# Decays beside the norm, SiLU inside the steps, a gate job behind four others, twelve blocks turned at the stage's end

## What is computed

```python
h = _rmsnorm(x, pre_g)
proj = jnp.einsum('bld,de->ble', h, w_in)
z_ssm, xbc, dt_raw, q, k, v, f_raw, z_att, g_ssm, g_att = jnp.split(proj, ...)
xbc = jax.nn.silu(_causal_dwconv(xbc, conv_w, conv_b))     # 2048 channels, 4 taps
xs, b_ssm, c_ssm = jnp.split(xbc, [1024, 1536], axis=-1)
dt = jax.nn.softplus(dt_raw + dt_bias)                     # 16 heads
a = -jnp.exp(a_log)
y = _ssd_chunked(xs, dt, a, b_ssm, c_ssm, d_skip)          # chunks of 128 tokens
yg = y * jax.nn.silu(z_ssm)
log_f = jax.nn.log_sigmoid(f_raw + fgate_b)                # 16 heads, summed along the tokens later
merged = jax.nn.sigmoid(g_ssm) * p_ssm + jax.nn.sigmoid(g_att) * p_att
```

## Time and profile before

| | us |
|---|---|
| median of 3 runs (3395.37 to 3403.71) | 3396.29 |
| the profiled execution's own time | 3377.47 |
| its span, first to last instruction | 3375.7 |
| TensorE matmul busy | 2890.9 (86%) |
| VectorE busy | 2027.7 (60%) |
| ScalarE busy | 1432.3 (42%) |
| GpSimd busy | 487.1 (14%) |
| mean granted TensorE clock | 0.925 of full |

### The profile page before, as it was taken

The page is one execution under the profiler, slowest core; times in us unless marked ns, Lnnn a source line. Parts: engine busy times, 40 slices in busy tenths (PEclk is TensorE's granted clock), DMA queues, the critical chain, the costliest instruction groups (busy, mean ns, idle before and its releaser), DMA issues. The chain is left out here.

```text
span 3375.7 us, 36680 instructions
## 1 busy us (share of the span) xinstructions
PE 2890.9 (86%) x13236; PEld 2310.3 (68%) x13236; DVE 2027.7 (60%) x2217; ACT 1432.3 (42%) x2086; POOL 487.1 (14%) x407
## 2 busy tenths in 40 slices
PE   6976887999997998799879975967999679999991
PEld 5865666788885766687768853654777568888881
DVE  3774545334443554345433989877345679999993
ACT  3341324333333666343333332343332257777770
POOL 0001310000002767000000000000000014434430
PEclk9986888999997999899989987989999879999996
DMA  3100010112446664112101100010111569999995
GB/s 88 44 19 4 0 36 15 57 50 94 150 143 147 128 134 97 57 51 93 63 20 44 50 14 1 1 38 13 56 44 44 189 246 391 378 378 378 375 338 228
DMA packets 220390, 396.26 MB, mean 117 GB/s; under 512 B 73313, under 2 KB 73441, under 8 KB 220256
## 3 DMA queue, kind: packets, MB, share of 16 engines
q1 hardware_dynamic: 211040, 377.66, 34.0%
q0 software_dynamic: 9216, 16.80, 1.3%
HBM read 356.32 MB, written 54.85 MB: 122 GB/s over the span
## 5 line engine op out<-in xcount | busy, mean ns | idle before, releaser
L2360 DVE TENSOR_TENSOR ex_w<-ex_raw,ex_w 128x2048 fp32r<-128x2048 f32 x192 | 436.6, 2290 | 49.2 <-ACT ex_w L2307 47.4
L2307 ACT ACTIVATE ex_w<-ex_raw 128x2048 fp32r<-128x2048 f32 x192 | 364.6, 1916 | 101.7 <-DMA ex_raw<-in_w_down_e 37.7
L2237 PE MATMUL ps<-ex_w,ex_xT 128*128 128x512 f32 x1536 | 366.7, 395 | 5.3 <-DVE ex_xT L2369 5.0
L2237 PEld LDWEIGHTS ps<-ex_w,ex_xT 128*128 128x128 f32 x1536 | 287.6, 189 | 67.7 <-DVE ex_xT L2369 6.5
L760 DVE TENSOR_TENSOR bs_t<-arena,bs_t 128x1024 fp32r<-128x1024 f32 x80 | 98.1, 1226 | 258.3 <-ACT bs_t L722 258.3
L613 DVE SCALAR_TENSOR_TENSOR arena<-arena,small 128x1023 f32<-128x1023 f32 (+9 forms) x168 | 213.7, 1272 | 4.3
L722 ACT ACTIVATE bs_t<-arena 128x1024 fp32r<-128x1024 f32 x80 | 84.9, 1061 | 296.9 <-PE ps L701 269.6
L699 PE MATMUL ps<-bs_t,bs_w 128*128 128x512 f32 x512 | 200.8, 392 | 11.1 <-DVE bs_w L763 9.0
L1063 POOL TENSOR_TENSOR fa_pl<-fa_p,fa_ph 128x512 fp32r<-128x512 f32 x192 | 191.7, 1012 | 100.8 <-ACT fa_ph L1180 97.9
L700 PE MATMUL ps<-bs_t,bs_w 128*128 128x512 f32 x512 | 200.0, 391 | 0.0
L701 PE MATMUL ps<-bs_t,bs_w 128*128 128x512 f32 x512 | 199.9, 390 | 0.0
(11 more groups left out here) (385 smaller groups left out, 6988.2 us busy)
## 6 DMA issues: line engine op xcount, KB each, us to landing
ex_raw<-in_w_gate_e SPq DMA_DIRECT2D x64, 1024.0 KB, 13.2
ex_raw<-in_w_up_e SPq DMA_DIRECT2D x64, 1024.0 KB, 13.2
ex_raw<-in_w_down_e SPq DMA_DIRECT2D x64, 1024.0 KB, 13.5
arena<-in_w_in SPq DMA_DIRECT2D x108, 512.0 KB, 3.6
arena<-in_x SPq DMA_DIRECT2D x4, 2048.0 KB, 11.2
arena<-in_w_out SPq DMA_DIRECT2D x16, 512.0 KB, 4.3
arena<-expert_out SPq DMA_DIRECT2D x8, 1024.0 KB, 12.2
arena<-in_w_branch_ssm SPq DMA_DIRECT2D x8, 512.0 KB, 3.6
```

The source lines that it names most:

```text
L2237: mm = nc.tensor.matmul(out, l, r, start=(k == 0 and n == 0), stop=(k == kc - 1 and n == 2))
L2307: nc.scalar.activation(half_of(part[m][0], h), raw[m][:, h * W // 2: (h + 1) * W // 2], ACT.Identity).then_inc(high[m], 1)
L2360: V.tensor_tensor(half_of(part[m][1], h), raw[m][:, h * W // 2: (h + 1) * W // 2], half_of(as_f32(part[m][0]), h), ALU.subtract)\
```

## The change

- The six loads of the decays are issued in the norm, behind the taps' and the biases'. In the norm TensorE also computes the logits of token tiles 0 to 4: those of tile t - 1 behind the transposes of tile t. The transposes use six banks in place of eight; bank 7 holds the logits.
- In xbc, the logits of tiles 5 to 7 stand ahead of the first step, and the bias add on VectorE behind them and ahead of its first splits. The small chain runs in steps 0, 2, 4 and 5 on VectorE and 1 and 3 on ScalarE. ScalarE applies SiLU to block b in step 2b + 10.
- xbc has a fifth job, the first half of the gate, which was bs's first job. All taps now lie inside the steps.
- At xbc's end twelve blocks are turned (C is left out), eight copied by VectorE, four (4, 6, 8, 10) by ScalarE, in three slots of two banks; the two sums are computed behind block 2, the exponentials behind the last copy.
- The stages turn of xbc and decays are gone. The forget sums are transposed and copied ahead of z's steps, scanned in its steps 0 to 3, and stored at its end. z's result goes to R(4) in place of R(2).

The core of the diff:

```diff
@@ phase_norm_T, TensorE
-                if n >= 8:
-                    pe.wait_ge(placed, n - 7)
+                if n >= 6:
+                    pe.wait_ge(placed, n - 5)
...
+                if h and 1 <= t <= decays.EARLY:
+                    pe.wait_ge(placed, 2 * t)
+                    decays.logit(pe, t - 1)
@@ class Decays (EARLY = 5)
+    def logit(self, pe, t):
+        n2 = 2 * HEADS
+        if t == 0:
+            pe.wait_ge(self.loaded, 96)
+        for k in range(KC):
+            mm = self.nc.tensor.matmul(self.ps[:, t * n2:(t + 1) * n2], self.hv[:, k, t * P:(t + 1) * P],
+                                       self.w[:, k, :], start=(k == 0), stop=(k == KC - 1))
+        mm.then_inc(self.logits, 1)
+
+    def on_tensor(self, pe):
+        for t in range(self.EARLY, TT):
+            self.logit(pe, t)
+        pe.wait_ge(self.step, 1)
+
+    def on_vector(self, dve):
...
+        dve.wait_ge(self.logits, TT)
+        self.st.then_wait(self.nc.vector.tensor_tensor(
+            v3(x), v3(self.ps), self.bias.unsqueeze(1).to_broadcast([P, TT, 2 * HEADS]), ALU.add))
@@ class TurnedBlocks (BLOCKS = 12, BY_ACT = (4, 6, 8, 10), SUMS = 6)
+    def on_tensor(self, pe, evicted):
+        c, nc, d = self.c, self.nc, self.decays
+        for b in range(self.BLOCKS):
+            slot = b % 3
+            pe.wait_ge(self.silued, b + 1)
+            if b < 3:
+                pe.wait_ge(evicted, XBC // BANK * TT + 2 * b + 2)
+            elif b - 3 in self.BY_ACT:
+                pe.wait_ge(self.by_act, self.BY_ACT.index(b - 3) + 1)
+            else:
+                pe.wait_ge(self.by_vec, self.on_dve.index(b - 3) + 1)
+            for t in range(TT):
+                mm = nc.tensor.transpose(c.ps[:, 2 * slot + t // 4, (t % 4) * P:(t % 4 + 1) * P],
+                                         self.av[:, b, t * P:(t + 1) * P], c.ident[:])
+            mm.then_inc(self.turned, 1)
+            if b == 2:
+                pe.wait_ge(evicted, XBC // BANK * TT + self.SUMS + 1)
+                pe.wait_ge(d.step, d.CHAIN)
+                nc.tensor.matmul(c.ps[:, self.SUMS, 0:P], c.upto[:], d.dta, start=True, stop=True)
+                nc.tensor.matmul(c.ps[:, self.SUMS, P:2 * P], c.ones[:], d.dta, start=True, stop=True)\
+                    .then_inc(self.summed, 1)
...
+    def on_scalar(self, act, tapped):
+        A, d = self.nc.scalar, self.decays
+        for b in self.BY_ACT:
+            act.wait_ge(self.turned, b + 1)
+            A.activation(*self.block(b), ACT.Identity).then_inc(self.by_act, 1)
+        act.wait_ge(d.step, d.ARGS)
+        A.activation(d.dte, d.dte, ACT.Exp).then_inc(d.act_step, 1)
+        A.activation(d.ecs, d.ncs, ACT.Exp, scale=-1.0).then_inc(d.act_step, 1)
+        A.activation(d.cdec, d.cdec, ACT.Exp).then_inc(d.act_step, 1)
@@ _build
+        def open_blocks(n, tapped):
+
+            decays.chain_on_scalar(n)
+            b, odd = divmod(n - KC - 2, 2)
+            if not odd and 0 <= b < XBC // P:
+                nc.scalar.wait_ge(tapped, CONV * (b + 1))
+                block = T(xbc_out, XBC // P)[:, b, :]
+                nc.scalar.activation(block, block, ACT.Silu).then_inc(turned.silued, 1)
+
         phase_dense(c, "xbc", [(T(R(0)), wcol(w_in, C_XBC, n), "act_T", wide(1 + n // 2, n % 2),
-                                ACT.Identity) for n in range(XBC // BANK)], 5,
-                    aside=convolve_xbc, trailing=KC)
-        phase_xbc_turn(c, xbc_out, xbc_in)
+                                ACT.Identity) for n in range(XBC // BANK)]
+                    + [(T(R(0)), wcol(w_in, C_GS, 0), "act_T", wide(2, 1), ACT.Sigmoid)], 5,
+                    aside=convolve_xbc, beside=open_blocks, begin=decays, end=turned)
...
-        phase_decays(c, R(0), a["w_in"][0], a["dt_bias"][0], a["a_log"][0], a["d_skip"][0],
-                     a["fgate_b"][0], att, R(5))
...
+        forget = ForgetSums(c, ctx, decays, R(1))
+        phase_dense(c, "z", [(T(R(0)), wcol(w_in, C_Z, n), "act", half(R(4), n), ACT.Silu)
+                             for n in range(2)], 5, begin=forget, aside=forget.aside,
+                    at_end=lambda sp, kept: forget.store(sp, att))
...
-        phase_dense(c, "bs", [(T(R(0)), wcol(w_in, C_GS, n), "act_T", wide(4, n), ACT.Sigmoid)
-                              for n in range(2)]
-                    + [(T(R(1)), wcol(a["w_branch_ssm"][0], 0, n), "mul_T", wide(2, n), wide(4, n))
-                       for n in range(2)]
+        phase_dense(c, "bs", [(T(R(0)), wcol(w_in, C_GS, 1), "act_T", wide(4, 1), ACT.Sigmoid)]
+                    + [(T(R(1)), wcol(a["w_branch_ssm"][0], 0, n), "mul_T", wide(2, n),
+                        wide((2, 4)[n], 1)) for n in range(2)]
```

More of the change, by code:

```diff
@@ L441 @@
-DTA_DONE, DECAY_ARGS, RUN_DONE = 14, 18, 22
-def phase_ssd(c, tok, bcT, y, tmp):
-    nc = c.nc
-    d = Decays(c)
+        self.forget = c.small[:, 1120:1120 + P]
+        n2 = 2 * HEADS
+        W = TT * n2
+        self.hv = hT.rearrange("p (k s) -> p k s", k=KC)
+        self.w = tmp[:, 0:KC * n2].rearrange("p (k n) -> p k n", k=KC)
+        self.wide = [tmp[:, 256 + j * W:256 + (j + 1) * W] for j in range(7)]
+        self.bias, self.a_neg = tmp[:, 2048:2048 + n2], tmp[:, 2080:2080 + HEADS]
@@ new lines, in __init__, with load @@
+        self.ps = c.ps[:, 7, 0:W]
+        self.loaded, self.logits = c.sem(ctx, "dec_loaded"), c.sem(ctx, "dec_logits")
+        self.step, self.act_step = c.sem(ctx, "dec_step"), c.sem(ctx, "dec_act")
+        self.st = Steps(self.nc.vector, self.step)
+    def load(self, sp, w_in, dt_bias, a_log, d_skip, fgate_b):
+        n2, wv = 2 * HEADS, cols(w_in)
+        with self.nc.allow_non_contiguous_dma(reason="narrow columns and broadcasts, once"):
+            for to, of in ((self.w[:, :, 0:HEADS], wv[:, :, C_DT:C_DT + HEADS]),
+                           (self.w[:, :, HEADS:n2], wv[:, :, C_F:C_F + HEADS]),
+                           (self.bias[:, 0:HEADS], bcast(dt_bias, HEADS)),
+                           (self.bias[:, HEADS:n2], bcast(fgate_b, HEADS)),
+                           (self.a_neg, bcast(a_log, HEADS)), (self.skip, bcast(d_skip, HEADS))):
+                sp.dma_start(to, of).then_inc(self.loaded, 16)
@@ new lines, in chain_on_scalar @@
+    def chain_on_scalar(self, n):
+        A, act = self.nc.scalar, self.nc.scalar
+        x, ax, e, u1, ln, eq, res = self.wide
+        if n == 1:
+            act.wait_ge(self.loaded, 96)
+            A.activation(self.a_neg, self.a_neg, ACT.Exp).then_inc(self.act_step, 1)
+            act.wait_ge(self.step, 3)
+            A.activation(e, ax, ACT.Exp, scale=-1.0).then_inc(self.act_step, 1)
+        elif n == 3:
+            act.wait_ge(self.step, 4)
+            A.activation(ln, u1, ACT.Ln).then_inc(self.act_step, 1)
@@ L618, in phase_dense @@
 def phase_dense(c, name, jobs, region, aside=None, trailing=0, move=(), made_by=None, gated_by=(),
-                fill=None, at_end=None, fetch=None, fetch_at=4, beside=None):
+                fill=None, at_end=None, fetch=None, fetch_at=4, beside=None, begin=None, end=None):
     nc = c.nc
@@ L685, in _ @@
         def _(pe):
+            if begin is not None:
+                begin.on_tensor(pe)
             for n, (j, k) in enumerate(steps):
@@ L709, in _ @@
                     pe.sem_inc(stepped, 1)
+            if end is not None:
+                end.on_tensor(pe, by_act)
         @block.scalar
@@ L741, in _ @@
                 if beside is not None:
-                    beside(n)
+                    beside(n, tapped)
                 j = steps[n - 1][0]
@@ L750, in _ @@
                     high_evict(j)
+            if end is not None:
+                end.on_scalar(act, tapped)
         @block.vector
@@ L764, in low_parts @@
                                 ALU.subtract).then_inc(w_low, 1)
+            if begin is not None:
+                begin.on_vector(dve)
             pairs = 0
@@ L799, in _ @@
                     x.then_inc(by_vec, 1)
+            if end is not None:
+                end.on_vector(dve)
 def phase_turn(c, name, src, dst, gate=None, groups=0, gain_dram=None, gain_times=1.0, width=D):
@@ L2499, in _build @@
         shifts = nc.dram_tensor("att_shifts", (HEADS, TT, P), F32).ap()
[L2500 to L2501 removed]
         if upto < 2:
             return c
[L2504 removed]
+        phase_ssd(c, decays, c.at(1, 0, TT * TOK), R(4), R(3), R(5))
         if upto < 3:
             return c
[L2508 to L2510 removed]
+        forget = ForgetSums(c, ctx, decays, R(1))
+        phase_dense(c, "z", [(T(R(0)), wcol(w_in, C_Z, n), "act", half(R(4), n), ACT.Silu)
+                             for n in range(2)], 5, begin=forget, aside=forget.aside,
+                    at_end=lambda sp, kept: forget.store(sp, att))
+        phase_turn(c, "y", R(3), R(1), gate=R(4), groups=GROUPS, gain_dram=a["ssm_norm_g"][0])
         if upto < 4:
@@ L2526, in fill_heads @@
             heads.fill_a(pool)
[L2527 removed]
+            pool.wait_ge(kept[7], 32)
```

(1 more changed line is left out.)

262 lines of the change are left out of this document (112 added, 150 removed).

## The result

The changed kernel takes **3347.95 us** (median of four executions, 3343.41 to 3349.2), the kernel before 3397.17 (3395.37 to 3403.71, four executions): a ratio of 0.9849 with a 95% interval of 0.9832 to 0.9866, or 49.2 us (1.5%). The forecast was 61.1 us less and 3335.2; the range 3318 to 3358 holds the result, and rival (a), the clock that stays at half through the norm, had said 3350. The profiled execution took 3349.2 us, its span 3347.4.

A forecast was written before the change was run, and what follows sets the result against it. Stage by stage: norm bound by VectorE, xbc by TensorE, decays a chain without overlap. Terms -77.3 + 14.6 + 3.0 - 1.4 = -61.1 us from the 3396.3 median gave 3335.2 us, range 3318 to 3358.

The forecast's parts named there:

- rival (a): Clock stays at half through norm and logits: norm +23.4 us, start of xbc +7.7, total 3350; chance 0.20.
- Parts 1 and 2: Gate job moved from bs to xbc, SiLU inside xbc's steps: net 0 each; the 15.5 us tail of taps goes.
- The margin of 0.8 us at the boundary: At xbc's job boundaries, evictions delayed by SiLU still fit by 0.8 us; otherwise three boundaries cost about 1 us each.
- Rival (d): Decays stay on the path, stretching xbc's first six steps by 7 to 12 us: 3345; chance 0.12 shared with mild late loads.
- Part 3: Turn at xbc's end: SSD starts 15.9 us after the last step; with the decays stage removed, saves 77.3 us.
- Part 4: Decays beside the norm: loads land at 31 us, TensorE waits for them, norm ends at 50.5 us, +14.6 us.
- between the two, I expect the rise after the second or third tile: In the norm's mix of logits and transposes, TensorE's clock rises from half to full at about 38 us.
- Rival (b): Early loads at 29.5 us and full clock throughout norm and logits: norm +9.5 us, total 3329; chance 0.15.
- The start of xbc: Three tiles' logits ahead of xbc's first matmul: it comes 8.6 us after the norm's end against 5.6, +3.0 us.
- The regained clock of the first step: xbc's first matmuls run at full clock if the logits keep it up: 2.6 us back, half taken, -1.4 us.
- Part 5: Forget sums in z fall into its wait for weights and idle time: 0 us, bounds -2.6 to +1.
- Rival (c): Decays' loads crawl behind tap loads, each microsecond after 31 costing one: 3345 mild; slower than before past 92, chance 0.015.

The follow-up runs named there:

- the second experiment: Changed kernel plus 52 identity transposes into an unused bank while TensorE waits for the decays' loads in the norm: median 3336.71 us, ratio 0.982.
- the first experiment: Changed kernel with the six loads of the decays issued ahead of the tap and bias loads: median 3336.87 us, ratio 0.9832.
- the long execution: Unedited re-profile of the kernel with loads first, seven tiles' logits in the norm and seventy transposes in the route stage: 3339.93 us.

## Why the prediction came out as it did

**Parts 1 and 2, gate job and SiLU: right.** Every step in between is 5.50 us, the boundaries show a gap of 0.30 us as the kernel before does, bs gave back what xbc took on, and taking the gate job back cost 15.5 us at the tail, the term's own number. The margin of 0.8 us at the boundary was not used up; the eight evictions behind the SiLU stand closer together. Rival (d), the first six steps stretched by the chain, did not happen: TensorE has no gap from 68.95 to the first boundary at 115.48.

**Part 3, the turn: right, 1.2 us too dear.** T + 14.75 for T + 15.9. ScalarE's copy of 1024 columns from PSUM is 1.02 us (taken: 1.06). From table load to the next activation it is 1.29 us, as in the earlier trace rows. The rule of the Trainium skill (ScalarE: Activation LUTs, What ACT_TABLE_LOAD costs) that adds a drain of 1.38 us is not borne out by this row either.

**Part 4, the loads: right; the clock: wrong.** The loads landed at 30.0 for 31, and TensorE waited 6.55 us for them. The step that failed is "between the two, I expect the rise after the second or third tile". It took two facts, logits alone don't raise the clock and transposes alone do, and put the mix between them. In the trace the mix stayed at 0.50 for all of its 27.2 us, which is rival (a). By its own bound, +23.4 with the loads at 31, the term comes to 22.4 with the loads at 30, and 22.0 was measured. The full-clock price of a tile's logits that no row of before had, 1.85 us, is shown now: 1.87, and with the tile's transposes 2.61 from start to start where the sum took 2.83. The mistake was in the transition, and the second experiment prices it: with the clock up at 30.5 the norm ended at 45.8, +9.9. That the result still lies in the range is because the range was drawn to take in rival (a); the forecast's own mechanism gave 3335, 13 us too little. Rival (b), early loads and full clock at 3329, is what the first experiment built: 3329.62 in the profiled execution, with the clock up in the norm, and 3330.39 in another.

**The start of xbc: +5.5 for +3.0.** Three tiles of logits were put at full clock (5.5 us) and took 8.33, since the clock fell 2.3 us into them. Rival (a) had them wholly at half clock, 10.3 us and +7.7; so did the profile of the kernel with the gate job taken back (10.42). The regained clock of the first step (-1.4) did not come for the same reason.

**Part 5: right.** z takes 96.1 us in both kernels, and the copy of 1.21 us lies in its wait for weights.

**Rival (c), late loads,** was closer to the point than its chance: that the loads land late is what made TensorE wait, and in the profiled execution the wait is what let the clock fall. The wait is not the only way to a low start, as the long execution without one shows. The rival's price was wrong, because it counted a microsecond of delay as one of time; logits that could start 6.4 us earlier (23.6 for 30.0) brought the first dense matmul forward by 17.6.

**What stays open.** From the last job of bs to the first of the next dense stage, the attention between them, it is 334.0 to 334.8 us in the three profiles of the kernel before with and without the route filler, and 335.9 to 339.0 in the changed kernel and the six made from it up to the one with the route filler. The difference of 1 to 5 us has no cause here, and the four later profiles, at 333.1 to 339.6, make part of it mere spread. Nor is it known when the clock comes up in the norm: in the sixteen transposes (3.29 and 3.31 us), behind them in the filler or in the first tile's logits (2.01 to 2.46), or not at all (3.59). And it is not known what makes the route's mix lose it.

## What to carry to other kernels

Before narrow float32 work is moved beside something else, ask at which clock TensorE will run it and its neighbours: put into a busy stretch it can share half clock with that stretch, and together with a wait for its loads it then cost more here than in one piece behind it. A wait ahead of such a mix can cost more than its own length: bring the loads forward first, and where that can't be done, a filler of transposes in the wait took half a microsecond here and saved eleven. Loads first do not make sure of the clock either: one profiled execution still started low. And hold one profile against the median of the runs before you take it as the base, then compare the pace of equal instructions, stage by stage, where it stands apart.

## What the runs showed of the hardware

- The same mix of eight transposes and sixteen narrow float32 instructions per tile has two lasting states: 27.2 us and 36.6 us at 0.50 (1.2 GHz), 14.2 and 20.0 us at 1.00 (2.4 GHz). Once the first tile's logits had run wholly at half clock, the mix did not leave the low state in any profile; in three norms the clock rose within the first tile's logits (2.01, 2.21 and 2.46 us). It left the high one in three of seven route stages that started high, in or right behind the second tile's logits, and in no norm.
- Under logits of 32 columns alone the clock went from 1.00 to 0.50, 2.3 us after 58.2 in the changed kernel, with TensorE busy without a gap in them, though behind one of 1.05 us. That gap alone doesn't explain it: the norm's transposes in the earlier trace rows kept full pace across gaps of 2.02 us. And 27.5 us of such logits did not raise the clock. The Trainium skill (TensorE: Matmul & The Clock Gate, Part 1) says that sustained matmul activity releases the throttle; for this shape the rows show busy time in which it did not rise and in which it fell.
- Work added to an engine made the program faster: 52 transposes by 11 us in the norm of the changed kernel, 70 transposes by 13 us in the route stage of the kernel before.
- A stage of one kernel took 76 or 93 us in two executions on identical work, enough to move the whole program by 0.5%.
